# The mLSTM's second product in plain float32, its projections reordered, and new durations in the planner of the order of work

## The reference, cut to what matters

```python
D = b[..., :, None] - b[..., None, :] + log_i[..., None, :]
D = jnp.where(tril, D, -jnp.inf)
g = b + m_prev[..., None]
m_t = jnp.maximum(g, jnp.max(D, axis=-1))
s = jnp.einsum('bhcld,bhcsd->bhcls', q, k) * jnp.exp(D - m_t[..., None])
inter = jnp.exp(g - m_t)
num = einsum(s, v) + inter[..., None] * einsum(q, C_prev)
den = jnp.sum(s, axis=-1) + inter * einsum(q, n_prev)
h = num / jnp.maximum(jnp.abs(den), jnp.exp(-m_t))
...
h_fwd = mlstm_chunkwise(q, k, v, i_fwd, log_sigmoid(f_fwd))
h_bwd = flip(mlstm_chunkwise(flip(q), flip(k), flip(v), ...))
hs = rms(h_fwd + h_bwd) * norm_w
return (hs * sigmoid(gate)) @ w_out
```

## Time and profile before

| | us |
|---|---|
| median of 3 runs | 1536.1 (1535.57 to 1537.43) |
| the profiled execution, its own time | 1534.96 |
| its span, first to last instruction | 1533.2 |
| PE busy in the span | 1459.8 (95%) |
| DVE busy | 855.2 (56%) |
| ACT busy | 597.9 (39%) |
| mean granted TensorE clock | 0.985 of full |

### The profile page before, as it was taken

The page is one execution under the profiler, slowest core; times in us unless marked ns, Lnnn a source line. Parts: engine busy times, 40 slices in busy tenths (PEclk is TensorE's granted clock), DMA queues, the critical chain, the costliest instruction groups (busy, mean ns, idle before and its releaser), DMA issues.

```text
span 1533.2 us, 18333 instructions
## 1 busy us (share of the span) xinstructions
PE 1459.8 (95%) x7200; PEld 1195.5 (78%) x7200; DVE 855.2 (56%) x1639; ACT 597.9 (39%) x1074; POOL 37.8 (2%) x43
## 2 busy tenths in 40 slices
PE   7999998998999789999999999999999999999996
PEld 6778795787888568888888887866678888888885
DVE  5677856566676665443344446487755453344433
ACT  5555533354445534232232333366654232222321
POOL 0011000000000000000000000000000000000000
PEclk9999998999999899999999999999999999999998
DMA  6121120041211103322323223210013322322221
GB/s 232 57 83 62 49 83 28 14 136 57 83 56 56 56 28 110 104 82 92 100 104 110 66 103 115 95 56 1 29 31 107 110 76 93 120 86 107 80 83 71
DMA packets 20901, 123.05 MB, mean 80 GB/s; under 512 B 2256, under 2 KB 2896, under 8 KB 9680
## 3 DMA queue, kind: packets, MB, share of 16 engines
q1 hardware_dynamic: 20816, 121.89, 23.3%
HBM read 119.78 MB, written 2.10 MB: 79 GB/s over the span
## 4 chain that ended last, share of the span: by engine, by line
PE 41%; issue 25%; DVE 6%; ACT 4%; DVEq 0%; POOLq 0%; POOL 0%; ACTq 0%
PE PS L231 38%; DVE FT L227 2%; PE PS L254 2%; PE PS L246 1%; ACT FR L206 1%; DVE FR L219 1%; ACT FT L206 1%; ACT WH L206 1%; DVE WL L219 1%; DVE FT L223 0%; DVE FT L219 0%; DVE G L219 0%; DVE SC L224 0%; ACT XH L206 0%; DVE XT L219 0%
## 5 line engine op out<-in xcount | busy, mean ns | idle before, releaser
L231 PE MATMUL PS<-XH,WH 128*128 128x512 f32 x1080 | 427.5, 396 | 0.0
L231 PE MATMUL PS<-XH,WL 128*128 128x512 f32 x1080 | 420.7, 390 | 0.0
L231 PE MATMUL PS<-XL,WH 128*128 128x512 f32 x1080 | 420.7, 390 | 0.0
L231 PE MATMUL PS<-FR,WH 128*128 128x512 f32 x1088 | 342.1, 396 | 15.0 <-DVE FR L219 9.2
L219 DVE TENSOR_TENSOR WL<-RAW,WH 128x1024 fp32r<-128x1024 f32 (+2 forms) x242 | 263.3, 1130 | 137.9 <-ACT WH L206 136.9
L206 ACT ACTIVATE WH<-RAW 128x1024 fp32r<-128x1024 f32 (+2 forms) x242 | 223.8, 973 | 141.2 <-PE PS L231 135.0
L231 PEld LDWEIGHTS PS<-FR,WH 128*128 128x128 f32 x1088 | 203.5, 190 | 63.3 <-issue 9.2
L231 PEld LDWEIGHTS PS<-XH,WH 128*128 128x128 f32 x1080 | 202.8, 188 | 47.9 <-issue 7.5
L231 PEld LDWEIGHTS PS<-XH,WL 128*128 128x128 f32 x1080 | 202.7, 188 | 43.0
L231 PEld LDWEIGHTS PS<-XL,WH 128*128 128x128 f32 x1080 | 202.9, 188 | 40.3 <-issue 0.5
L231 PE MATMUL PS<-FR,WL 128*128 128x512 f32 x544 | 213.6, 393 | 0.0
(11 more groups left out here) (113 smaller groups left out, 1278.5 us busy)
## 6 DMA issues: line engine op xcount, KB each, us to landing
RAW<-in_f_in SPq DMA_DIRECT2D x44, 1024.0 KB, 4.9
RAW<-in_w_in SPq DMA_DIRECT2D x13, 1024.0 KB, 4.9
RAW<-in_m_in SPq DMA_DIRECT2D x12, 1024.0 KB, 4.9
RAW<-in_f_oa SPq DMA_DIRECT2D x16, 768.0 KB, 4.4
RAW<-in_f_ob SPq DMA_DIRECT2D x16, 640.0 KB, 3.8
RAW<-in_a_in SPq DMA_DIRECT2D x6, 1024.0 KB, 5.0
RAW<-in_w_out SPq DMA_DIRECT2D x4, 1024.0 KB, 4.9
RAW<-in_m_out SPq DMA_DIRECT2D x4, 1024.0 KB, 4.9
```

The costliest lines, as they stand in the source:

```text
L231: f = lambda e: e.matmul(o, l, r, start=start, stop=stop, skip_group_check=True)
```

## The change

Two things are changed together. In the mLSTM, the exponentials times scores and the values are kept in plain float32: `outp` makes one plain float32 matmul of 258 columns for each pair in place of three; `part` writes its product straight into one FP buffer and `split` is gone there; values are evacuated by one ACT copy, with no low part; VF holds all four heads; the constant ones beside the values are one memset; a head holds 5 buffers of FR and not 10. The chunks come in another order (M_ORDER) and m_turn waits for its head's output gate while the order is built. Second, the durations and lags from which `weave` builds the order are others, in all three woven stages.

```diff
+LAG = {"pe": 0.24, "ac": 0.07, "dv": 0.07, "po": 0.1, "sp": 0.07}
...
-        WHEN[self.name, self.n] = self.t + 0.07
+        WHEN[self.name, self.n] = self.t + LAG[self.name]
...
-        us = 0.1 + 0.00083 * width(o) + (0 if accum is None else 0.19)
+        us = 0.19 + 0.00083 * width(o) + (0 if accum is None else 0.19) + (0 if isinstance(scale, float) else 0.09)
...
     def dve_us(o):
-        return 0.07 + 0.00104 * width(o)
+        return 0.15 + 0.00104 * width(o)
...
+    def pe_us(l, w):
+        return max(0.107, (w + 32) / 2400) / (2 if l.shape[0] <= 64 else 1)
...
-        us = 0.00042 * width(o)
+        us = pe_us(l, width(o))
...
-        us = 4 * 0.00042 * width(o) if us is None else us
+        us = 4 * (width(o) + 4) / 2400 if us is None else us
...
-    for c in range(12):
-        chunks.append((A["m_in"][c], 8, 256))
+    M_ORDER = ("q0", "v0", "q1", "v1", "g0", "q2", "v2", "g1", "q3", "v3", "g2", "g3")
+    for c in M_ORDER:
+        chunks.append((A["m_in"][3 * int(c[1]) + "gvq".index(c[0])], 8, 256))
...
-                    op0=ALU.add, op1=ALU.min, accum_out=nm), t, tb, sf, us=0.6)
+                    op0=ALU.add, op1=ALU.min, accum_out=nm), t, tb, sf, us=0.77)
...
+        V = VF[:, :].rearrange("p (s i n) -> p s i n", s=4, i=4)
+        tv = DV.op(lambda e: e.memset(V[:, :, :, 256:258], 1.0), vv_free)
...
-                toks += v_evac(b, t, V[:, s, 0, i, 0:256], V[:, s, 1, i, 0:256], i, 256,
-                               [ready.get(("mpv", hd - 2)), vv_free])
+                    t1 = copy(V[:, hd, i, 0:256], PS[:, b, 0:256], t, st["rct"], vv_free, scale=st["rc"][:, i:i + 1])
...
-                tg = stt(FT[:, p, w], FT[:, p, w], st["rc"][:, kt:kt + 1], PS[:, b, w], ALU.mult, ALU.mult, te, t, st["rct"])
...
-                tk = split(FT[:, p, w], FR[:, hb, w], FR[:, lb, w], tg, hf, lf)
+                tg = stt(FP[:, gb, w], FT[:, p, w], st["rc"][:, kt:kt + 1], PS[:, b, w], ALU.mult, ALU.mult, te, t, st["rct"], gf)
...
-                    mm(PS[:, b, 0:258], FR[:, hb, c], vh, kt == ks[0], False, tk, ready["mv", hd], fb)
-                    mm(PS[:, b, 0:256], FR[:, hb, c], vl, False, False)
-                    t = mm(PS[:, b, 0:258], FR[:, lb, c], vh, False, kt == ks[-1])
+                    gb, tk = x["gtok"][d, kt]
+                    t = mm4(PS[:, b, 0:258], FP[:, gb, c], V[:, hd, kt, :], kt == ks[0], kt == ks[-1], tk, ready["mv", hd], fb)
...
     def m_turn(hd, i, f, tok):
+        while ("g", 2 * hd + 1) not in ready:
+            yield None
+        yield tok
```

More of the change, by code:

```diff
@@ L1115, in m_proj @@
         vv_free = st["vv_free"]
[L1116 to L1132, removed]
-                for i in range(4):
[L1134 to L1142, removed]
-                toks += v_evac(b, t, V[:, s, 0, i, 0:256], V[:, s, 1, i, 0:256], i, 256,
-                               [ready.get(("mpv", hd - 2)), vv_free])
-            ready["mv", hd] = toks + ready["vone", s]
-            w_done[j] = t
-            while len(fr.q) < 4 + st.get("fr_kept", 10):
@@ new lines, in m_proj @@
+        V = VF[:, :].rearrange("p (s i n) -> p s i n", s=4, i=4)
+        tv = DV.op(lambda e: e.memset(V[:, :, :, 256:258], 1.0), vv_free)
+        for c in M_ORDER:
+            hd = int(c[1])
+            if c[0] == "g":
+                j, h, l, wt = w_use()
+                for u in range(2):
+                    yield from fm_tile(h, l, wt, u * 128)
+                    b, t = st["pb"], st["pt"]
+                    g = 2 * hd + u
+                    gate_tile(b, t, g, ACT.Sigmoid)
+                    ready["g", g] = ts(G[:, g, :], G[:, g, :], SM[:, C_MLN + g:C_MLN + g + 1], ALU.mult, ready["g", g], t_sm)
+                w_done[j] = t
+                continue
+            if c[0] == "v":
+                j, h, l, wt = w_use()
+                toks = [tv]
+                for i in range(4):
+                    b, fb = bank.take()
+                    yield from proj_tm(h, l, wt, i, b, fb)
+                    t = st["pt"]
+                    t1 = copy(V[:, hd, i, 0:256], PS[:, b, 0:256], t, st["rct"], vv_free, scale=st["rc"][:, i:i + 1])
+                    bank.put(b, t1)
+                    toks.append(t1)
+                ready["mv", hd] = toks
+                w_done[j] = t
+                ready["m", hd] = True
+                continue
+            while len(fr.q) < 4 + st.get("fr_kept", 5):
@@ L1153, in m_proj @@
                 b, t = st["pb"], st["pt"]
+                if hd == 0 and u == 0:
+                    norm_bcast()
+                    ready["mgate"] = (bg, tg)
                 (fh, f1), (fl, f2) = got[u]
@@ L1169, in m_proj @@
             w_done[j] = t
-            ready["m", hd] = True
         st["xfree"] = t
@@ L1214, in part @@
                 w = slice(128 * kt, 512) if d == 0 else slice(0, 128 * kt + 128)
-                tg = stt(FT[:, p, w], FT[:, p, w], st["rc"][:, kt:kt + 1], PS[:, b, w], ALU.mult, ALU.mult, te, t, st["rct"])
-                rd.append(tg)
                 n = kt if d == 0 else kt + 1
                 if n not in x["gt"]:
-                    x["gt"][n] = (fr.take(), fr.take())
-                    st["fr_kept"] -= 2
-                (hb, hf), (lb, lf) = x["gt"][n]
-                tk = split(FT[:, p, w], FR[:, hb, w], FR[:, lb, w], tg, hf, lf)
-                ft.put(p, tk)
-                x["gtok"][d, kt] = (hb, lb, tk)
+                    x["gt"][n] = fr.take()
+                    st["fr_kept"] -= 1
+                gb, gf = x["gt"][n]
+                tg = stt(FP[:, gb, w], FT[:, p, w], st["rc"][:, kt:kt + 1], PS[:, b, w], ALU.mult, ALU.mult, te, t, st["rct"], gf)
+                rd.append(tg)
+                ft.put(p, tg)
+                x["gtok"][d, kt] = (gb, tg)
             bank.put(b, rd)
@@ L1264, in outp @@
                 st["vv_free"] = t
-                for a_, b_ in x["gt"].values():
+                for a_ in x["gt"].values():
                     fr.put(a_[0], t)
-                    fr.put(b_[0], t)
-                st["fr_kept"] = 10 if hd < 3 else 0
+                st["fr_kept"] = 5 if hd < 3 else 0
             return hd, i, f, [t2, tb], pw
@@ L1277, in m_heads @@
                 yield None
-            while len(fr.q) < 10:
+            while len(fr.q) < 5:
                 yield None
-            st["fr_kept"] = 10
+            st["fr_kept"] = 5
             rows(hd)
@@ L1285, in m_heads @@
                 if i == 1 and o2 is not None:
-                    yield o2[3]
-                    m_turn(*o2)
+                    yield from m_turn(*o2)
                     o2 = norm(*o1)
                 if i == 3 and o2 is not None:
-                    yield o2[3]
-                    m_turn(*o2)
+                    yield from m_turn(*o2)
                     o1 = o2 = None
@@ L1294, in m_heads @@
                 g = H[hd]["gtok"]
-                yield [g[d, kt][2] for d in range(2) for kt in (range(0, i + 1) if d == 0 else range(i, 4))]
+                yield [g[d, kt][1] for d in range(2) for kt in (range(0, i + 1) if d == 0 else range(i, 4))]
                 n1 = outp(hd, i)
@@ L1464, in stage1 @@
                 x = DV.op(lambda e, o_=o_, i_=i_, a_=a_: e.tensor_tensor_reduce(
-                    out=o_, in0=i_, in1=mask, scale=1.0, scalar=-NEG, op0=ALU.add, op1=ALU.min, accum_out=a_), t, sf, t_co, us=0.45)
+                    out=o_, in0=i_, in1=mask, scale=1.0, scalar=-NEG, op0=ALU.add, op1=ALU.min, accum_out=a_), t, sf, t_co, us=0.23 + 0.00104 * width(o_))
                 bank.put(b, x)
```

14 lines of the change are left out of this document (4 added, 10 removed).

## The result

| | before | after |
|---|---|---|
| median (range), 7 runs each | 1536.1 (1535.46 to 1537.43) | **1542.47** (1539.85 to 1544.56) |
| the profiled execution, its span | 1534.96, 1533.2 | 1544.18, 1542.4 |
| PE busy, DVE, ACT in the span | 1459.8, 855.2, 597.9 | 1473.2, 834.5, 583.1 |
| mean granted TensorE clock | 0.985 | 0.975 |

The account below looks back on a forecast made before the run. PE was taken to bound the kernel, busy 1459.8 us of the span. The mLSTM's -15 (21 back, 6 paid) and -9 in block 1 and attention made -24: 1511 from 1534.96, as a median 1512 us, range 1499 to 1525.

Parts of the forecast that it names:

- The second product, +6 us: mLSTM: 80 plain float32 matmuls at 0.435 us take 34.8 us on PE against 29.0 before, +6 us.
- The weight loads' rival: mLSTM: 160 float32 records each load weights in view at 0.15 us, 24 us, leaving 1536 us; chance 0.04.
- The gates, -2 us: mLSTM to 372 us: the wait for ncol stays, scans still priced at 0.6 us; 2 of 7.2 us back.
- The middle and the last head, -4 and -15 us: mLSTM, 372 to 505: work before early turns, 4 us back; 505 to 580: more cover, no splits, 15 of 19.7 back.
- Block 1 and attention, -9 us: Order alone changes: 4 of 13.7 us back in block 1's second part, 1 before 205, 4 of 9.4 in attention.
- The half price on 64 rows: Block 1: the new table takes a single retention head on 64 partitions at half of what PE needs; no size given.
- The rival of the other side: Attention: items without projections make PE wait and its clock fall, some 40 us lost, 1552 us; chance 0.04.
- normalisation under 4 us: Sign in the mLSTM: PE's waits for normalisation fall from 13 us to under 4.
- the last stretch under 6 us idle: Sign in the mLSTM: the stretch behind the last projection has under 6 us idle and no clock of 0.5.
- wrong if block 1 or attention lose more than 3 us: Sign against the forecast: block 1 or attention losing more than 3 us would show it wrong.

Follow-up runs that it names:

- e10: As e1, but the four scans of the gates are priced at 1.21 us in place of 0.6: 1515.65 us.
- e3: The changed kernel planned with the old durations in all three woven stages: 1525.34 us.
- e4: As e1, but the mLSTM's chunks come in the old order g, v, q: 1524.98 us.
- e12: The changed kernel's block 1 with chunk v0 ahead of r1, the mLSTM of e10, the attention with old durations: 1521.73 us.
- e9: As e1, but matmuls on 64 rows are planned at half price in block 1 and attention: 1534.13 us.
- e7: The changed kernel with all new durations except the half price of matmuls on 64 rows: 1527.76 us.
- e11: As e1, but with DVE's new price added to the old durations in block 1, and PE's new lag alone in attention: 1533.06 us.
- e2: The kernel before with nothing but the new durations and lags, in all three woven stages: 1560.21 us.
- e8: The changed kernel with DVE's fixed price back at 0.07 in place of 0.15 us, all else new: 1536.17 us.
- e1: The changed kernel with block 1 and attention ordered by the old durations, the mLSTM by the new ones: 1519.29 us.
- e5: The changed kernel, all new durations, with the side stream counted as ready 2 us early in block 1 and attention: 1538.51 us.

## Why the prediction was wrong

- **The second product, +6 us: right.** 0.423 to 0.436 us for one, where 0.435 was taken; five pairs 2.12 to 2.18 us against 1.81, sixteen groups, +5 to +6 us. The long groups lie below the 0.430 us that the prediction gave as the least, so a distance from start to start is good to 0.1 us for a group and no more. The weight loads' rival is out: its 0.15 us for each record, 0.30 for a pair, would show beside 0.43. "TensorE: Matmul & The Clock Gate" of the Trainium skill (Wait — 56ns, not 53.3ns?) would give 0.440 us for four passes; the trace, at 0.423 to 0.436, is below it.
- **The gates, -2 us: right in what stays.** ncol was waited for, once, 3.5 us, as said. e10 shows the cause named there, the scans priced at 0.6 us: 4.3 us of the stage for four numbers.
- **The middle and the last head, -4 and -15 us: right in sum.** The length less PE's busy time went from 27.4 to 9.6 us in the whole mLSTM, -17.8, and the low clock shrank with it. The stage: -17.2, forecast -15. How it is shared: 11 by the unsplit product and the order of chunks (e3), 5 to 6 by the durations; the order of chunks is worth some 3 of the whole, measured with the new durations (e4).
- **Block 1 and attention, -9 us: this step failed.** It was +16.3 and +7.0. Its reasons were that the order in block 1 changes "by groups of 3 to 18 matmuls only" and that new durations nearer to the trace bring a better order; the bounds allowed 3 us worse. Neither held. The first was said of block 1's second part alone, and the largest wait came ahead of it, where the prediction expected 1 us back: the order changed by 39 matmuls at the one place where they were cover (30 between scores and turn, 6 and 3 behind), and I had looked at the order of the retention and the attention, not at the heads of differential attention, since before showed no waits there. Having no wait was not a reason to leave the place out: it was cover that could be lost. And the quality of durations is not what decides in block 1. `weave` takes what is ready by its clock and never holds a projection back; what decides is how far the projections run ahead, and whether they stand still at a chunk that needs a buffer. The shown chain is: new durations, projections further ahead, r1 without buffers, a wait of 6.7 us and its clock (e12).
- **The half price on 64 rows** was named there as "against it", at no price. It is enough to make the hole (e9: 306.1) and without it there is none (e7: 300.6), but so is DVE's price alone (e11: 309.7). Naming a wrong number in a table does not tell the sign of what it does; that needs the order.
- **The rival of the other side**, items without projections in the attention and the low clock behind them, was right in kind and had its place in the wrong stage for the most. It was weighed at 0.04 and priced at 40 us; there it cost 7 (5.3 idle, 1.7 clock), and in block 1, where cover was lost in the same way, the stage lost 16.3.
- **Of the signs named**: normalisation under 4 us, yes (0.2); the last stretch under 6 us idle, nearly (500 to 592.47 has 92.47 less 86.38, 6.1); "wrong if block 1 or attention lose more than 3 us", yes.

In the attention the cause is known only to this point: the new durations bring it in every kernel that has all or nearly all of them there (13.1 to 13.4 us idle after, in e2, e7 and e8; 7.8 with the old ones in before, e1, e3, e4, e10, e12), and neither the half price alone (e9: 8.6 us idle) nor PE's lag alone (e11: 9.5) brings it. Taking the side stream 2 us earlier removes most of it (e5: 8.9). Its chunks of q wait for FR buffers by the same loop, and the planner's steps point the same way: counting the instructions by which PE tells others that it is done, the last chunk of q first finds no buffers behind the 401st in before and e1, the 397th in e9 and e11, and the 391st in after, e2, e7 and e8. So the same cause is likely, but no run changed that, and it stays open.

## What to carry to other kernels

Where a greedy planner fills one engine with two streams, a change of its numbers is a change of every stage it plans, and more exact numbers are no promise of a better order: build it, and for each stretch count the cover between the producer and the consumer of every long chain, first of all where the profile of before shows no wait. Look for the place at which the filling stream must stand still (a buffer, a bank, a turn), and put in front of it the piece of work that needs none of that. And price a lost cover twice: the wait, and the low clock behind it.

## What the runs showed that was not expected

- **The same order does not always get the same clock back.** In the attention of e1 the instructions and waits of PE are those of before. Before, after a wait of 3.1 us for ACT, the windows are

```profile
1030.00:1035.00 5.00, 2.58 (x12) 1.24 (x12) 4.07 (x21) 3.44 (x13) 0.00 (x0) 0.68 0.43 180
1035.00:1040.00 5.00, 5.00 (x32) 3.53 (x31) 3.68 (x20) 4.06 (x16) 0.00 (x0) 0.98 0.01 3
```

and in e1

```profile
1015.00:1020.00 5.00, 2.48 (x12) 1.24 (x12) 3.98 (x20) 3.53 (x13) 0.00 (x0) 0.68 0.45 187
1020.00:1025.00 5.00, 5.00 (x19) 3.84 (x18) 2.48 (x12) 3.55 (x13) 0.00 (x0) 0.50 0.00 0
1025.00:1030.00 5.00, 5.00 (x18) 3.03 (x18) 2.31 (x10) 0.89 (x4) 0.00 (x0) 0.50 0.00 0
1030.00:1035.00 5.00, 5.00 (x28) 3.63 (x28) 3.49 (x14) 3.99 (x14) 0.00 (x0) 0.96 0.00 0
```

PE did the same before both falls; in one case it had 2.4 GHz again within 5 us, in the other it stayed at 1.2 GHz for 10 us more, which is the 5.6 us by which the two stages differ. In the same way block 1 of after and of e2, the same order, is 314.4 and 307.6, and a stage with gaps is not known better than to some 5 us by one profile. What makes the one or the other isn't settled here. Of the 16.3 us of block 1 the waits are the sure part (7.8), the clock (8.4) varies. But it isn't chance alone: all seven runs of after have a mean clock of 0.974 to 0.976 and took 1539.85 to 1544.56 us, and e2's other three runs, at 0.971 or 0.972, were 3 to 7 us slower than its profiled one at 0.974.
- **Scores on 64 rows: six matmuls take as long as three.** The six of a pair of heads, on the two halves of the partitions, took 0.90 us before (169.53 to 170.43, above). The three of a single head in the retention, of the same 64 rows and 512 columns, took 0.89:

```profile
229.85 0.96 PE L231 MATMUL PS<-FR 64*128 64x512 f32 x3
230.74 0.96 PE L231 MATMUL PS<-FR,VV 128*128 128x512 f32 x3
```

So the two halves run side by side, and a single head gains nothing by its 64 rows; both are some 0.2 us over three matmuls of 0.227. The planner's 0.215 us for each is too much for a pair (1.29) and too little for a single head (0.65); its 0.113 is too little for both (0.68 and 0.34).
